# A streaming encoder block on one core: 192 tokens by row gathers, activations and remainders interleaved, remainders on GpSimd, V in 8 KB runs

## What is computed

```python
q = (xf @ w_pq).reshape(t, PEER_HEADS, 2, PEER_HALF)
sc = jnp.einsum("thpd,hpnd->thpn", q, sub_keys)
vals, idx = lax.top_k(sc, PEER_TOPK)
...
eidx = jnp.take_along_axis(cidx, pos, axis=-1)       # 8 heads x 16 experts of each token
g = jax.nn.softmax(best, axis=-1)
...
act = jax.nn.gelu(jnp.einsum("td,tkd->tk", xt, u[eidx]), approximate=False) * gt
out = jnp.einsum("tk,tkd->td", act, v[eidx])
```

## Time and profile before

| | us |
|---|---|
| median of 3 runs (1619.15 to 1621.73) | 1620.82 |
| span of the profiled execution | 1618.1 |
| TensorE busy | 1570.4 (97%) |
| VectorE busy | 1403.7 (87%) |
| ScalarE busy | 641.8 (40%) |
| GpSimd busy | 624.0 (39%) |
| transfers over the span | 436.11 MB, mean 270 GB/s |
| the sweep | about 717 to 1606 |

### The profile page before, as it was taken

How to read it: one execution, slowest core, us unless ns; L and a number is a source line. 1 busy time by engine, 2 the same in 40 slices (tenths; PEclk the granted TensorE clock), 3 DMA queues, 4 the chain that set the end, 5 groups by cost and what they waited for, 6 DMA issues and landing times.

```text
span 1618.1 us, 23763 instructions
## 1 busy us (share of the span) xinstructions
PE 1570.4 (97%) x7899; PEld 1291.7 (80%) x7899; DVE 1403.7 (87%) x2781; ACT 641.8 (40%) x955; POOL 624.0 (39%) x531
## 2 busy tenths in 40 slices
PE   6999999999999999999999999999999999999997
PEld 3777764665557899988888888898888888888886
DVE  6888877764999999979888998989999998989886
ACT  4234654241122666663333333333333333333233
POOL 0000000010555500016655666656555676767520
PEclk8999999989999999999999999999999999999998
DMA  8432215542212355589999999999999999999981
GB/s 349 167 150 79 79 52 197 221 155 78 92 72 73 106 205 199 209 307 402 402 380 386 375 380 389 394 392 387 355 396 358 387 362 398 347 380 355 403 301 64
DMA packets 127851, 436.11 MB, mean 270 GB/s; under 512 B 12832, under 2 KB 35360, under 8 KB 122016
## 3 DMA queue, kind: packets, MB, share of 16 engines
q1 hardware_dynamic: 74112, 247.92, 41.2%
q0 software_dynamic: 52224, 184.62, 29.6%
q10 hardware_dynamic: 1440, 2.62, 0.4%
HBM read 407.29 MB, written 27.79 MB: 269 GB/s over the span
## 4 chain that ended last, share of the span: by engine, by line
PE 71%; DVE 19%; DMA 4%; issue 3%; ACT 2%; POOL 0%; DVEq 0%; SPq 0%; ACTq 0%; POOLq 0%
PE ps L970 23%; PE ps L900 23%; PE ps L671 10%; PE ps L662 6%; PE ps L958 3%; DMA graw<-gmat 3%; PE ps L827 3%; DVE low L1886 2%; DVE Vs L1874 1%; DVE Us L1857 1%; DVE big L1886 1%; DVE att L1713 1%; DVE att L1724 1%; DVE big L1711 1%; DVE big L1729 1%
## 5 line engine op out<-in xcount | busy, mean ns | idle before, releaser
L970 PE MATMUL ps<-Vs,As 128*128 128x512 f32 x2286 | 535.6, 390 | 2.5 <-DVE As L1877 2.5
L970 PEld LDWEIGHTS ps<-Vs,As 128*128 128x128 f32 x2286 | 425.9, 188 | 86.1 <-DVE Vs L1874 1.6
L900 PE MATMUL ps<-xs,Us 128*128 128x336 f32 x2832 | 461.2, 318 | 5.1 <-DVE Us L1857 4.2
L900 PEld LDWEIGHTS ps<-xs,Us 128*128 128x128 f32 x2832 | 441.4, 188 | 22.6 <-issue 10.0
L594 POOL DMA_INDIRECT big<-pv,islot x176 | 255.9, 1454 | 144.6 <-DVE low L1916 50.9
L1338 ACT ACTIVATE big<-ps 128x352 f32<-128x352 f32 x96 | 44.7, 465 | 340.4 <-PE ps L900 281.2
L1874 DVE TENSOR_TENSOR Vs<-big,Vs 128x1024 fp32r<-128x1024 f32 x127 | 155.2, 1222 | 17.1 <-ACT Vs L1344 14.3
L662 PE MATMUL ps<-big 128*128 128x512 f32 (+1 forms) x416 | 160.3, 544 | 1.3 <-ACT big L1040 1.3
L1916 DVE SCALAR_TENSOR_TENSOR low<-big,low 128x1024 f32<-128x1024 f32 x128 | 157.0, 1280 | 0.0
L1344 ACT ACTIVATE Vs<-big 128x1024 fp32r<-128x1024 f32 x127 | 134.0, 1055 | 42.9 <-PE ps L970 40.7
L594 POOL DMA_INDIRECT low<-pu,islot x88 | 119.7, 1360 | 72.5 <-DVE colv L1886 53.9
(11 more groups left out here) (249 smaller groups left out, 2087.2 us busy)
## 6 DMA issues: line engine op xcount, KB each, us to landing
big<-puT SPq DMA_DIRECT2D x128, 512.0 KB, 3.5
big<-pv SPq DMA_DIRECT2D x64, 1024.0 KB
big<-stream SPq DMA_DIRECT2D x31, 1024.0 KB, 5.2
gmat<-big SPq DMA_DIRECT2D x11, 2048.0 KB, 7.3
graw<-gmat SPq DMA_DIRECT2D x30, 512.0 KB
low<-wada SPq DMA_DIRECT2D x28, 512.0 KB, 4.8
work<-wada SPq DMA_DIRECT2D x14, 512.0 KB, 5.6
graw<-gmat SPq DMA_DIRECT2D x15, 384.0 KB
```

What stands on the lines that cost most here:

```text
L900: mm = nc.tensor.matmul(ps[:, 6 + e, DEAD:ET], a, xs[:, b, k, :], start=(k == 0 and a is hi and b == 0), stop=(k == KT - 1 and a is lo))
L970: mm = nc.tensor.matmul(ps[:, 2 * b + half, :], a, v_parts[:, w, half * T:(half + 1) * T], start=(opens and a is hi and w == 0), stop=(las ...
```

## The change

- `NEXT` is 4: 64 extra tokens and so 192 tokens go by rows, with 192 gathers of U and 192 of V (`UB` = 62, `VE` = 124). The dense part has 320 columns everywhere; nothing in it is dead, and the clearing matmuls and zero fills are gone. The table takes 80 turns and 10 pieces.
- The rounded A and its remainder are interleaved (`As` of 640 columns, even and odd, `a_part`). Block 0 of the dense tokens has 64 left; its stationary operand is now 128 columns in a row, 64 tokens with rounded part and remainder side by side, and it needs two products instead of three. Blocks 1 and 2 read every second column (a step of two) and keep three. An output is 16 matmuls.
- The two halves of block 0's result are added at the end: ScalarE copies the banks (`unfolded`), and two matmuls with `fold` add neighbouring rows (`fold_halves`). The blocks are finished in the order 0, 2, 1, 3.
- The remainder of A is formed by GpSimd (`rest_a`), whose loop is written out: one remainder, then the gathers that the dots or adds of that step make room for. The copy of indices is gone.
- V is laid out in pairs of tiles, so that a load has one run of 8 KB for each partition.

```diff
 EXT = 16
-NEXT = 3
+NEXT = 4
 XTOK = EXT * NEXT
 NROWS = XTOK + SLOTS
-UB = 60
-VE = 122
+UB = 62
+VE = 124
...
-DEAD = XTOK - XB
+HALF = P - XB
+ORDER = (0, 2, 1, 3)
...
-        As = sb("As", [P, 2, 2, DT], f32r)
+        As = sb("As", [P, 2, 2 * ET], f32r)
...
+        def a_part(A, w):
+
+            return A.rearrange("p (t w) -> p w t", w=2)[:, w, :]
...
+        def dots_by(o):
+
+            return NROWS * min(max(o - 1, 0), UB - 2) // (UB - 2)
+
+        def adds_by(o):
+
+            return NROWS * min(max(o - UB + 1, 0), VE - UB) // (VE - UB)
+
+        def taken_by(o):
+
+            return dots_by(o) + adds_by(o)
...
-                sp.dma_start(vraw[:, e % 2, :, :],
-                             pv[bass.ds((g * BODY + 2 * e) * P, 2 * P), :].rearrange("(a p) f -> p a f", p=P)
+                sp.dma_start(vraw[:, e % 2, :, :].rearrange("p a f -> p (a f)"),
+                             pvP[bass.ds(g * (BODY // 2) + e, 1), :, :].rearrange("a p f -> (a p) f")
                              ).then_inc(v_here[e % 2], 16)
...
-            def fetch(table, places, it, r0, first=False):
...
+            def fetch(r):
+
+                if r >= ROWBUF:
+                    pool.wait_ge(row_used, r - ROWBUF + 1)
+                if r == NROWS:
+                    pool.wait_ge(alo_ready, EVERY * (-(-4 * D // ET)) + 3)
+                table, places, c = (pu, u_row, r) if r < NROWS else (pv, v_row, r - NROWS)
+                nc.gpsimd.indirect_dma_start(
+                    out=places[c % ROWBUF], out_offset=None, in_=table,
+                    in_offset=bass.IndirectOffsetOnAxis(ap=eidx[:, c:c + 1], axis=0)
+                    ).then_inc(row_here[r % ROWBUF], 16)
+
+            def rest_a(o):
+
+                A = As[:, o % 2, :] if o < XT - 1 else Al
+                if o % EVERY == EVERY - 1:
+                    act_t = early[:, o // EVERY, :]
+                else:
+                    act_t = gel[:, (o - o // EVERY) % 2, :]
+                pool.wait_ge(ahi_ready, o + 1)
+                nc.gpsimd.tensor_tensor(a_part(A, 1), act_t, a_part(A, 0).bitcast(f32), ALU.subtract).then_inc(alo_ready, 1)
...
-            with pool.Fori(1, NROWS // (2 * DOTS)) as it:
-                fetch(pu, u_row, it, 0)
-            pool.wait_ge(alo_ready, EVERY * (-(-4 * D // DT)) + 3)
-            with pool.Fori(0, NROWS // (2 * DOTS)) as it:
-                fetch(pv, v_row, it, NROWS)
+            for r in range(ROWBUF):
+                fetch(r)
+            r = ROWBUF
+            for o in range(XT):
+                rest_a(o)
+                while r < 2 * NROWS and r - ROWBUF < taken_by(o):
+                    fetch(r)
+                    r += 1
...
-            def clear(e):
-
-                nc.tensor.matmul(ps[:, e, 0:DEAD], zeros[:, :], ones[:, 0:DEAD], start=True, stop=True)
-
-            clear(0)
-            clear(1)
...
             def output_block(o, b, a_parts, v_parts, last=False, opens=False):
-                hi, lo = (a_parts[:, w, b * P:(b + 1) * P] for w in range(2))
-                for a, w in ((hi, 0), (hi, 1), (lo, 0)):
+                if b == 0:
+                    both = a_parts[:, 0:P]
+                    pairs = ((both, 0), (both, 1))
+                else:
+                    hi, lo = (a_part(a_parts, w)[:, HALF + (b - 1) * P:HALF + b * P] for w in range(2))
+                    pairs = ((hi, 0), (hi, 1), (lo, 0))
+                for i, (a, w) in enumerate(pairs):
                     for half in range(2):
                         mm = nc.tensor.matmul(ps[:, 2 * b + half, :], a, v_parts[:, w, half * T:(half + 1) * T],
-                                              start=(opens and a is hi and w == 0), stop=(last and a is lo))
+                                              start=(opens and i == 0), stop=(last and i == len(pairs) - 1))
+                return mm
+
+            def fold_halves(src, part, begins=False, ends=False):
+
+                for half in range(2):
+                    mm = nc.tensor.matmul(ps[:, 6 + half, :], part, src[:, half * T:(half + 1) * T],
+                                          start=begins, stop=ends)
                 return mm
...
+                        pe.wait_ge(unfolded_ready, 1)
+                        fold_halves(unfolded, fold, ends=True).then_inc(folded, 1)
...
+            f(unfolded, ps[:, 0:2, :].rearrange("p h d -> p (h d)"), ACT.Copy).then_inc(unfolded_ready, 1)
...
-                A, V = (As[:, a, :, :], Vs[:, a, :, :]) if o < XT - 1 else (Al, Vl)
+                V = Vs[:, a, :, :] if o < XT - 1 else Vl
                 dve.wait_ge(vhi_ready, o + 1)
                 v.tensor_tensor(V[:, 1, :], vraw[:, d // 2 % 2, d % 2, :], V[:, 0, :].bitcast(f32), ALU.subtract
                                 ).then_inc(vlo_ready, 1)
-                dve.wait_ge(ahi_ready, o + 1)
-                v.tensor_tensor(A[:, 1, XB:DT], act_t, A[:, 0, XB:DT].bitcast(f32), ALU.subtract).then_inc(alo_ready, 1)
...
+                    dve.wait_ge(folded, 1)
```

176 lines of the change are left out of this document (86 added, 90 removed).

## The result

The changed kernel takes 1649.34 us (median of 4 runs, 1647.87 to 1649.88) where the kernel before takes 1620.16 us beside it (4 runs): a ratio of 1.0177, 95% interval 1.0162 to 1.0191. It is slower, as forecast, but by 29.2 us and not by 8. The profiled execution has a span of 1646.9 us, 28.8 more than before's 1618.1. The forecast of 1629 was 20 us short, and the time lies just inside the end of its range, 1650.

A forecast was written before the change was run, and what follows sets the result against it. TensorE was taken to bound the kernel before. After, VectorE's 850 us (GpSimd 837, transfers 823, TensorE 769) plus 2% gave 867; with 12 behind, against 864.5, -7, +0.7 and 2.7 for the median: 1629 us, range 1597 to 1650.

The forecast's parts named there:

- TensorE's part: Sweep: output products fall to 3.63 us, hidden ones to 3.55, a step to 6.29 us, 0.57 less.
- rival 3: Output matmuls: the strided stationary operand slows TensorE, deciding near 290 ns a matmul; above 1640 us, chance 0.04.
- The port: Sweep: each remainder on GpSimd stops VectorE through their shared SBUF port, for 0.72 us (0.63 to 0.85).
- The forecast's sum for VectorE: First dot to last added row: dots, adds, other work and port stops ask 850 us of VectorE.
- 2% of friction: First dot to last added row: VectorE, GpSimd and transfers waiting for one another lose 2%, making 867 us.
- -7 us: Loop before the sweep: four turns fewer and shorter hidden products let the sweep start 7 us earlier.
- GpSimd's step: Sweep: gathers and one remainder take GpSimd 6.73 us a step beside dots, 6.98 beside adds, 837 in all.
- rival 2: Sweep: GpSimd is the bound if its gathers become 0.15 us longer each; 1657 us, chance 0.10.
- 5 us of "others": TensorE's sum for the kernel before, first dot to last hidden product: work besides output and hidden products, 5 us.
- +0.7 at the end: End of the kernel: block 0's fold runs beside other blocks' output, the first residual comes later; + 0.7 us.
- The transfers: First dot until the last row is there: 334 MB at 406 GB/s take 823 us.
- Rival 1: Sweep: the port costs little and the transfers are the bound; 1597 us, faster, chance 0.25.

The follow-up runs named there:

- experiment 6: Changed kernel with rounded activations and remainders each in one contiguous run instead of interleaved: 1650.04 us, ratio 1.0196.
- experiment 1: Changed kernel with GpSimd's first two remainders of A ahead of the first eight gathers, the third between the fourth and fifth: 1642.42 us, ratio 1.0156.
- experiment 9's control: Kernel before with its adds spread over four more steps, until step 125 in place of 121: 1620.08 us, ratio 1.0011.
- experiment 5: Changed kernel with remainders of A on VectorE up to step 62, on GpSimd only beside the adds: 1622.17 us, ratio 1.0018.
- experiment 2: Changed kernel with all remainders of A back on VectorE: 1612.95 us, ratio 0.9961.
- experiment 9: Changed kernel with remainders of A on VectorE and rows spread over two more steps, until step 125: 1602.88 us, ratio 0.9905.
- the fastest version: Changed kernel with remainders of A on VectorE, rows until step 125, boundary between dots and adds at 65: 1601.94 us, ratio 0.9881.

## Why the prediction was wrong

**TensorE's part was right.** Output products were forecast at 3.63 us and took 3.73, hidden ones at 3.55 and took 3.51. The six ns of the strided load I had costed at nothing are the 0.1; they decided nothing (experiment 6), as rival 3's low chance had it. The page of the Trainium skill that I had set beside that rival (SBUF — State Buffer, section Door 1: The DMA port swizzle: fp32 may step by four at full rate) differs from the trace by these six ns in 227, and is right on what they mean for the time.

**The port was right, near its value.** I took 0.72 us a remainder between 0.63 and 0.85 (my own proportion gives 0.71); the trace shows 0.67 in the dots and 0.60 in the adds. The forecast's sum for VectorE holds in the half where VectorE is the bound: 62 steps of 2.42 + 0.60 us, 242 us of adds, less one step's other work, which lies ahead of the first add, are some 426 us; 425.1 were measured. There I had added a needless 2% of friction and 0.12 us of port, and forecast about 450 us for the steps with adds and the weights between. The Trainium skill (SBUF — State Buffer, section Who interferes with whom) says that the lock is held for the whole instruction. Here a remainder takes 0.85 us with VectorE idle (two in 1.71 us at 729.75 above), its record beside the dots is 1.10 us, and VectorE loses 0.67: the measurement gives less than the rule. Why it is less no run shows.

**The step that failed first: the start of the sweep was taken as unchanged.** My sum ran from the first dot to the end of the last hidden product and moved the start by -7 us. I had listed GpSimd's queue for the steps, but not the one place where the first remainder stands behind eight gathers and a wait for the stored pieces. The first dot came 13.7 us later than before, 20.7 later than the sum had it. Experiment 1 shows the cause of 13.3 of them. It also shows that undoing it is worth 7 us of time or less, since the steps behind take part of it back. The rows for this stood in the trace of before: 11.3 us from the first gather to the end of the eighth, and output(0) begun at 717.92, ahead of them. The other 7 us are the shorter loop before the sweep. TensorE's first output did come 7 us earlier in experiment 1 (710.95), but the first dot never did: it stands at 728.5 to 733.5 us in the five versions whose GpSimd starts with gathers alone, at 729.9 in experiment 1, and at 729.5 and 731.7 in the kernel before and in experiment 9's control. So the term of -7 was not there to be had at the place where the sum used it; which wait holds the first dot in each version I didn't take apart.

**The second: GpSimd's step was sized with gathers too short.** 3.2 x 1.62 + 1.55 = 6.73 us was the sum in the dots; VectorE's 6.80 stood just above it. A gather took 1.59 us and not 1.32, so 3.2 x 0.27 = 0.86 more; the remainder took 1.10 with hardly any issue time, 0.45 less; 7.14 us. The stretch of dots shows (433.6 - 5) / 60 = 7.14. VectorE's own sum is 6.08 + 0.67 = 6.75, not far below. This is rival 2, by its own rule (gathers 0.15 us longer each) in half of the sweep: 17 us lost there against VectorE's remainders, and 5 beside the adds, the 17 in a proportion of queue and port that stays open (experiment 5). I gave it 0.10 and let it decide over the whole sweep or not at all, which put its price at 1657. I had even read the sign of it: V's gathers at 1.45 us beside U's 1.32. What I hadn't seen is that the average mixes two kinds: between 800 and 1130 us the 56 gathers of before that began behind a wait for a dot took 1.15 us on average, the 87 others 1.43. After the change only 7 waited; 101 others took 1.54 and the 39 directly behind a remainder 1.74. (In experiment 2's kernel the 55 behind a wait took 1.57 and the others 1.42, so a wait ahead doesn't make a gather short everywhere.)

**The third: the fold's new place.** I had 5 us of "others" in TensorE's sum for before and 3 in the one for after, and +0.7 at the end. The fold is 6.9 us, and now behind the last hidden product where nothing covers it; from that product's end to the span's end 31.5 us pass, before 24.1. Within the forecast this was hidden by luck, an error of the other sign: from the first dot to the end the forecast had 15.2 us more than before, and 15.1 were measured, with the dots 12 us longer than forecast (428.6 for 416), weights and adds 20 shorter (431 for 451) and the tail 7 longer. A sum that comes out right can be right for no good reason.

**The transfers** were sized right: 406 GB/s is the most that the version with VectorE's remainders reaches, and it stays near it (399 to 406 in the windows of experiments 2 and 9, 384 to 390 where dots give way to adds). Rival 1 (the transfers as the bound, 1597 us) names what most likely bounds that version (at 1613 us), not this one.

What stays open: how the 17 us beside the dots divide between GpSimd's queue and the port; why no version starts its dots earlier than before by the 7 us; whether the fold can be covered again (its banks are taken until the last hidden product); and how much of the 17 us between the fastest version and the kernel before belongs to fewer passes of TensorE, and how much to gathers without index copies. I ran nothing that parts these two.

## What to carry to other kernels

When work is moved to an engine with slack on average, cost it in that engine's own program order: what stands ahead of its first instance, and whether the engine is full in any one stage. GpSimd, busy for half of the span, had a stage here in which it waited for others for 8 of 330 us. A duration taken while an engine mostly waits can be too short for the same engine when it is full: here 1.32 against 1.59 us. And when an edit shifts the bound, retune the numbers that were set for the old one: spreading the rows was worth nothing before and 10 us after.

## What the runs showed of the hardware

- A gather on GpSimd takes 0.94 us with VectorE idle (728.78 above) and 1.3 to 1.6 on average beside VectorE's dots, single ones from 0.94 up to 2.0 us. It happens where GpSimd computes nothing else too (1.44 and 1.50 us in experiment 2). That VectorE's hold on the shared port is the cause was only argued.
- A GpSimd subtraction with two operands of 128x320 costs VectorE 0.60 to 0.67 us for a record of 1.08 to 1.10, and takes 0.85 with VectorE idle. A copy with one operand of the same size (0.68 us) still made 30 of VectorE's instructions 0.26 us late.
- Stationary operands with a step of two elements of 4 bytes in 12 of 16 matmuls of 512 columns: one starts every 233 ns instead of 227.
- Transfers held 401 to 406 GB/s at a share of 1.02 to 1.03 over stretches of 160 to 200 us (experiment 9), not only for the 20 us of the earlier trace rows.
